# Beginning of a two-layer encoder trunk on one Trainium2 core: x in eight pieces, the first two weight units in halves and computed together, the third unit's split weights in other buffers

## The chip, the cores and the metric

The kernel runs on one core of a Trainium2 chip. The metric is device time in microseconds for one launch. In this document PE is TensorE, ACT is ScalarE, DVE is VectorE, POOL is GpSimd and SP is SyncE, which issues most of the DMAs.

## The reference

Input x is 512 tokens by 1024 features, float32. There are two layers and a final RMSNorm:

```python
for layer in range(DEPTH):
    h = rms_norm(x, norm_mix[layer])
    if layer % 2 == 0:      # one projection, then a gated linear-attention head group and a
        x = x + mixer_gla_sb(h, ab_w_in[i], ab_w_gate2[i], ab_b_gate[i], ab_gla_norm[i], ab_w_out[i])
    else:                   # stick-breaking group; or windowed attention with sinks and a bias
        x = x + mixer_swa(h, c_w_qkv[i], c_sinks[i], c_w_out[i], rel_bias)
    h = rms_norm(x, norm_ffn[layer])
    x = x + conv_ffn(h, ffn_w_up[layer], ffn_conv_w[layer], ffn_conv_b[layer], ffn_w_down[layer])
return rms_norm(x, norm_final)

def rms_norm(x, g):
    return x * lax.rsqrt(jnp.mean(x * x, axis=-1, keepdims=True) + EPS) * g
```

This case touches only the start of layer 0: `rms_norm` and the first of the 25 weight units of `h @ ab_w_in[0]`, namely the first 128 columns each of the stick-breaking q and k (`("qb", 0)`, `("kb", 0)`) and a quarter of its v (`("vb", 0)`).

## The kernel before, in words

**Layout.** x is held transposed, as `x[128, 8, 512]`: eight chunks of 128 features, each with 512 tokens in a row. Weights come in units of 128x1024 float32 (512 KB). A q or k unit is "stationary": eight 128x128 blocks, one per chunk of x. A v unit is "moving": two chunks of weight rows with 512 columns each.

**Three products for one.** Every product is computed as three float32r matmuls. A tensor t is split into `hi` (an ACT copy to float32r) and `lo` (DVE: t minus hi), and hi*hi + hi*lo + lo*hi is accumulated in PSUM; the function is `three`, lines 1160 to 1162. A unit makes 24 matmuls of 512 columns. A weight unit u is loaded by SP into `w_raw[u % 4]`, split by ACT into `w_hi[u % 2]` and by DVE into `w_lo[u % 2]`. Because there are two split buffers, ACT waits for `unit_done` to reach u - 1 before it writes unit u (`hi`, line 599 to 601); DVE's part is `lo` (line 840).

**The norm.** The projection works on x times gain, without 1/rms: ACT writes `h_hi` (line 632), DVE `h_lo` (line 855). Meanwhile the row sums of squares are built: ACT squares the eight chunks (`sq`, line 651), DVE adds each into `ssq` (`add_sq`, line 850), PE sums `ssq` over the partitions (`ssq_mm`, line 1206), and DVE, POOL and PE turn that into `rinv` (lines 873, 588, 877, 1213), by which results are scaled as they leave PSUM.

**Order.** `mix0_order` makes one list of steps, `SEQ0`, and PE, ACT and DVE each walk it and do their part of each step. A step `("unit", u, (a, b))` is eighths a to b of a unit. Behind the last eighth of unit u, `with_splits` puts a step `("split", u)`, at which ACT and DVE split unit u + 2. Before the change the list begins: q's chunks 0 to 3, k's chunks 0 to 3, squares of chunks 0 to 3, q's chunks 4 to 7 and split 0, squares of 4 to 7, k's chunks 4 to 7 and split 1, the whole unit vb 0 and split 2, then `ssq`. The two first units (q, k) are split ahead of the list by two loops over the chunks, on ACT (lines 624 to 632) and on DVE (lines 883 to 886).

**Loads.** At the start SP issues weight unit 0, x chunks 0 and 1, weight unit 1, x chunks 6 and 7, weight units 2 and 3; ACT issues all small parameters (`par`, 202 KB) and then x chunks 2 and 3, and 4 and 5. A row of the table of DMAs below is one of these. PE runs 14 matmuls on a constant (line 1278) while it waits. A queue works through its own DMAs in order; both queues share the 16 DMA engines. Unit 4 and later wait for `w_lo_ready`.

Of the kernel before, what the change touches and what calls it, by code (L numbers as in the profile page):

```python
# [27 lines left out]
F32 = mybir.dt.float32  # L28
# [3 lines left out]
ALU = mybir.AluOpType  # L32
# [3 lines left out]
T = 512  # L36
# [82 lines left out]
def mix0_order():  # L119
# [3 lines left out]
    def ev(name, i=0):  # L123
        return [(name, i, None)]
# [10 lines left out]
    q, k = unit("qb"), unit("kb")  # L135
    seq = q[:4] + k[:4] + ev("sq", 0) + q[4:] + ev("sq", 1) + k[4:]
    seq += unit("vb", 0) + ev("ssq") + cut("vb", 1, 6, "rinv")
# [95 lines left out]
def trunk(nc, xT, w_mix0, w_mix1, w_up, w_down, small, wg2, bias, out):  # L233
    ctx = ExitStack()
    with ctx:
# [3 lines left out]
        def sem(name):  # L239
            return ctx.enter_context(nc.semaphore(name))  # L240
# [24 lines left out]
        def s0(name, shape, dt=F32):  # L265
            return sb(name, shape, dt, m0)
# [20 lines left out]
        sbH = s0("sbH", [P, ZN], F32R)  # L287
        sbL = s0("sbL", [P, ZN], F32R)
        gE = s0("gE", [P, TT * GH * GK])
        gL = s0("gL", [P, TT * GH * GK])  # L290
# [57 lines left out]
        unit_done = sem("unit_done")  # L348
        x_loaded = [sem(f"x_loaded{i}") for i in range(4)]
        par_loaded = sem("par_loaded")  # L350
# [134 lines left out]

        def x_pair(i):
            return xT[:, 2 * i * T:(2 * i + 2) * T].rearrange("p (c t) -> p c t", t=T)

# [18 lines left out]
        def _(sp):  # L507
# [7 lines left out]

            for u in range(RAW):
                sp.dma_start(w_raw[u][:, :], w_mix0[u]).then_inc(w_loaded[u], 16)
                if u < 2:
                    i = 3 * u
                    sp.dma_start(x[:, 2 * i:2 * i + 2, :], x_pair(i)).then_inc(x_loaded[i], 16)  # L520
            sp.dma_start(wg2_sb[:, :], wg2).then_inc(wg2_loaded, 16)
# [72 lines left out]
        def _(act):  # L594
# [23 lines left out]

            act.dma_start(par[:, :], small).then_inc(par_loaded, 16)
            for i in (1, 2):  # L620
                act.dma_start(x[:, 2 * i:2 * i + 2, :], x_pair(i)).then_inc(x_loaded[i], 16)


            for c in range(KC):
                if c % 4 == 0:
                    act.wait_ge(w_loaded[c // 4], 16)
                    s.activation(w_hi[c // 4][:, :], w_raw[c // 4][:, :], ACT.Copy).then_inc(w_hi_ready, 1)
                if c == 0:
                    act.wait_ge(par_loaded, 16)
                if c % 2 == 0:  # L630
                    act.wait_ge(x_loaded[c // 2], 16)
                s.activation(h_hi[:, c, :], x[:, c, :], ACT.Copy, scale=gain_at(0, c)).then_inc(hi_ready, 1)


# [6 lines left out]
            for name, i, span in SEQ0:  # L641
                if name == "unit" and span[1] == 8:
                    n, part = MIX0[i]
                    if n in B_PARTS and part == B_PARTS[n] - 1:
                        act.wait_ge(unit_done, i + 1)
                        b_evac({"vb": vb, "va": va, "kg": kg}[n], B_COLS[n], b_tile, a_before(MIX0, i))
                elif name == "split":
                    hi_static(i + SPL)
# [59 lines left out]
            def ffn(layer, norm, u_up, u_dn, r0, next_cols, last):  # L708


                act.wait_ge(warmed, layer)
                s.activation(gelu_warm[:, :], par[:, 0:1], ACT.Gelu_apprx_tanh).then_inc(warmed, 1)

# [120 lines left out]
        def _(dve):  # L834
# [46 lines left out]

            v.memset(ssq[:, :], 0.0).then_inc(ssq_added, 1)
            for c in range(KC):
                if c % 4 == 0:
                    lo_static(c // 4)
                h_lo_part(0, c)
            dve.wait_ge(consts, N_CONSTS)
            v.tensor_copy(ident_bf[:, :], ident[:, :]).then_inc(consts_dve, 1)
# [17 lines left out]
            for name, i, span in SEQ0:  # L906
                if name == "unit" and span[1] == 8:
                    if i >= 2 and MIX0[i][0] not in B_PARTS:
                        a_evac0(i)
                elif name == "split":  # L910
                    lo_static(i + SPL)
# [243 lines left out]
        def _(pe):  # L1155
# [11 lines left out]

            def a_unit(u, r, bank, h_blocks=None, span=(0, KC)):

                if span[0] == 0:  # L1170
                    pe.wait_ge(w_lo_ready, u + 1)
                for c in range(*span):
                    if h_blocks is not None:
                        pe.wait_ge(lo_ready, h_blocks + c + 1)
                    ins = three(ps[:, bank, :], w_blocks(r, c), (h_hi[:, c, :], h_lo[:, c, :]),
                                c == 0, c == KC - 1)
                if span[1] == KC:
                    ins.then_inc(unit_done, 1)

            def b_unit(u, part, parts, tile, n_cols, span=(0, 8), a_taken_by=None):  # L1180
# [5 lines left out]
                for step in range(span[0] * steps // 8, span[1] * steps // 8):  # L1186

                    half, rest = divmod(step, steps // 2)
                    k, tt = rest // 2, 3 - 2 * half - rest % 2
                    c = part * blocks + k  # L1190
                    if a_taken_by is not None and c == 0 and tt == 1:
                        pe.wait_ge(a_taken, a_taken_by)
                    tok = slice(tt * P, (tt + 1) * P)

                    ins = three(tile(tt, n_cols), (h_hi[:, c, tok], h_lo[:, c, tok]), w_blocks(u % RAW, k, n_cols),
                                c == 0 and (tile is b_tile or tt % 2 == 1), c == KC - 1, tile is v_tile)
# [84 lines left out]
            for at, (name, i, span) in enumerate(SEQ0):  # L1281
                if name == "unit":
# [10 lines left out]
                    else:  # L1293
                        if a >= 4 and span[0] == 0:
                            pe.wait_ge(a_taken, a - 1)
                        if b_done and span[0] == 0:
                            after_group = MIX0[i - 1][0] in B_PARTS
                            pe.wait_ge(b_taken, b_done - TT + 1 if after_group else b_done)
                        a_unit(i, i, a_bank0(a), 0 if i < 2 else None, span)
                elif name == "ssq":  # L1300
# [266 lines left out]
```

## Time and profile before

| | us |
|---|---|
| median of 3 runs | 1163.75 (1162.48 to 1165.25) |
| the profiled execution, its own time | 1162.42 |
| its span in the trace | 1160.7 |
| PE busy in the span | 1127.6 (97%) |
| DVE busy, ACT busy | 653.8 (56%), 492.8 (42%) |

The span leaves out 1.7 us around it. Busy time of PE includes the overlap of pipelined matmuls (a 512-column matmul is shown as 0.39 us long, and the next one starts 0.23 us later), so starts, not durations, tell the pace.

### The profile page before, as it was taken

The page shows a single profiled execution, that of the slowest core. Times are in us where ns is not written, and L with a number is a line of the kernel's source. Part 1 is how long each engine was busy: PE and PEld are TensorE (multiplying, and loading weights), DVE is VectorE, ACT ScalarE, POOL GpSimd, SP SyncE. Part 2 cuts the span into 40 slices and gives each one's busy share as a digit, 9 for nine tenths or more (in the row PEclk, how much of TensorE's full clock was granted, in tenths as well). Part 3 has the DMA queues.
Part 4 walks back from the last instruction along what each step waited for, and adds up shares of the span by engine and source line. Part 5 has one row for each costly group of instructions (what it writes and reads, how often), then busy time and mean ns, then how long its engine had stood idle before and what let it go on. Part 6 is the DMA issues. An engine that isn't in the chain of part 4 may idle for free.

```text
span 1160.7 us, 15078 instructions
## 1 busy us (share of the span) xinstructions
PE 1127.6 (97%) x5402; PEld 918.6 (79%) x5402; DVE 653.8 (56%) x837; ACT 492.8 (42%) x714; POOL 8.6 (1%) x25
## 2 busy tenths in 40 slices
PE   8999999999999999999999999899999999999995
PEld 7776777778888888888888777688888888888884
DVE  6324343565777777774333565655777777763333
ACT  5547354843434434443332365634443443432220
POOL 1000000000000000000000000000000000000000
PEclk9999899999999999999999999999999999999997
DMA  5211111122232232223333222132222223233331
GB/s 225 73 55 55 55 55 55 55 91 91 91 107 92 90 106 93 90 77 94 94 99 120 98 73 89 38 104 89 98 90 103 95 90 106 77 85 93 97 86 72
DMA packets 31751, 102.92 MB, mean 89 GB/s; under 512 B 3537, under 2 KB 3682, under 8 KB 31714
## 3 DMA queue, kind: packets, MB, share of 16 engines
q1 hardware_dynamic: 30978, 100.17, 26.2%
q10 hardware_dynamic: 736, 2.24, 0.6%
q8 instruction: 25, 0.41, 0.1%
q14 instruction: 12, 0.10, 0.0%
HBM read 99.84 MB, written 2.10 MB: 88 GB/s over the span
## 4 chain that ended last, share of the span: by engine, by line
PE 59%; issue 32%; ACT 5%; DVE 4%; DMA 1%; POOLq 0%; POOL 0%; ACTq 0%; DVEq 0%; SPq 0%
PE ps L1160 17%; PE ps L1162 17%; PE ps L1161 17%; PE ps L1324 2%; PE ps L1311 2%; ACT pr L817 1%; ACT w_hi L601 1%; PE ps L1333 1%; DVE w_lo L840 1%; DMA x<-xT 1%; PE ps L1456 1%; DVE sc L1111 1%; ACT sbE L663 0%; DVE mx L1121 0%; DVE x L1148 0%
## 5 line engine op out<-in xcount | busy, mean ns | idle before, releaser
L601 ACT ACTIVATE w_hi<-w_raw 128x1024 fp32r<-128x1024 f32 (+1 forms) x203 | 198.1, 976 | 512.9 <-PE ps L1162 512.9
L840 DVE TENSOR_TENSOR w_lo<-w_raw,w_hi 128x1024 fp32r<-128x1024 f32 (+1 forms) x205 | 229.8, 1121 | 243.7 <-ACT w_hi L601 237.8
L1160 PE MATMUL ps<-h_hi,w_hi 128*128 128x512 f32 x896 | 355.6, 397 | 8.2 <-DVE h_lo L855 3.1
L1162 PE MATMUL ps<-h_hi,w_lo 128*128 128x512 f32 x896 | 349.6, 390 | 0.0
L1161 PE MATMUL ps<-h_lo,w_hi 128*128 128x512 f32 x896 | 349.6, 390 | 0.0
L1160 PEld LDWEIGHTS ps<-h_hi,w_hi 128*128 128x128 f32 x896 | 168.6, 188 | 48.1 <-issue 11.6
L1162 PEld LDWEIGHTS ps<-h_hi,w_lo 128*128 128x128 f32 x896 | 168.6, 188 | 35.4
L1161 PEld LDWEIGHTS ps<-h_lo,w_hi 128*128 128x128 f32 x896 | 168.7, 188 | 35.0 <-issue 1.2
L1160 PE MATMUL ps<-y_hi,w_hi 128*128 128x512 f32 x352 | 136.9, 389 | 0.0
L1161 PE MATMUL ps<-y_lo,w_hi 128*128 128x512 f32 x352 | 136.9, 389 | 0.0
L1162 PE MATMUL ps<-y_hi,w_lo 128*128 128x512 f32 x352 | 136.9, 389 | 0.0
L988 DVE TENSOR_TENSOR us<-ps,rinv 128x512 f32<-128x512 f32 x88 | 60.7, 692 | 84.7 <-PE ps L1162 84.7
L1160 PEld LDWEIGHTS ps<-y_hi,w_hi 128*128 128x128 f32 x352 | 66.1, 188 | 13.8
L1162 PEld LDWEIGHTS ps<-y_hi,w_lo 128*128 128x128 f32 x352 | 66.1, 188 | 13.8
L1161 PEld LDWEIGHTS ps<-y_lo,w_hi 128*128 128x128 f32 x352 | 66.1, 188 | 13.5
L998 DVE SCALAR_TENSOR_TENSOR cv<-us,par,cv 128x512 f32<-128x512 f32 x88 | 66.2, 752 | 11.0 <-DVE cv L995 0.6
L725 ACT ACTIVATE cv<-us,par 128x512 f32<-128x512 f32 x88 | 70.6, 804 | 2.9 <-DVE us L988 2.9
L995 DVE SCALAR_TENSOR_TENSOR cv<-us,par,cv 128x512 f32<-128x512 f32 x88 | 65.6, 746 | 0.6 <-ACT cv L725 0.6
L861 DVE TENSOR_TENSOR x<-ps,x 128x512 f32<-128x512 f32 (+1 forms) x32 | 22.1, 691 | 56.2 <-PE ps L1162 56.2
L1160 PE MATMUL ps<-w_hi,h_hi 128*128 128x512 f32 (+2 forms) x128 | 45.3, 354 | 2.7 <-DVE kbT L900 2.6
L1162 PE MATMUL ps<-w_hi,h_lo 128*128 128x512 f32 (+2 forms) x128 | 43.8, 342 | 0.0
L1161 PE MATMUL ps<-w_lo,h_hi 128*128 128x512 f32 (+2 forms) x128 | 43.8, 342 | 0.0
(181 smaller groups left out, 1050.6 us busy)
## 6 DMA issues: line engine op xcount, KB each, us to landing
w_raw<-w_up SPq DMA_DIRECT2D x88, 512.0 KB, 3.2
w_raw<-w_mix SPq DMA_DIRECT2D x53, 512.0 KB, 3.3
w_raw<-w_down SPq DMA_DIRECT2D x32, 384.0 KB, 3.1
w_raw<-w_down SPq DMA_DIRECT2D x32, 320.0 KB, 2.9
out<-x SPq DMA_DIRECT2D x8, 256.0 KB, 2.2
x<-xT SPq DMA_DIRECT2D x2, 512.0 KB, 8.0
x<-xT ACTq DMA_DIRECT2D x2, 512.0 KB, 8.7
bias_sb<-bias ACTq DMA_DIRECT2D x1, 512.0 KB, 3.9
```

The costliest lines, as they stand in the source:

```text
L601: s.activation(w_hi[r % SPL][:, 0:cols], w_raw[r][:, 0:cols], ACT.Copy).then_inc(w_hi_ready, 1)
L725: s.activation(cv[k % 4][:, :], us[k % 2][:, 2:2 + T], ACT.Identity, bias=par[:, bass.ds(taps + 3, 1)], scale=par[:, bass.ds(taps + 2, 1)] ...
L840: v.tensor_tensor(w_lo[r % SPL][:, 0:cols], w_raw[r][:, 0:cols], w_hi[r % SPL][:, 0:cols].bitcast(F32), ALU.subtract).then_inc(w_lo_ready, 1)
L861: v.tensor_tensor(blk(x, c), ps[:, bank, :], blk(x, c), ALU.add).then_inc(x_updated, 1)
L988: v.tensor_tensor(us[k % 2][:, 2:2 + T], ps[:, k, :], rinv[:, :], ALU.mult).then_inc(u_scaled, 1)
L995: v.scalar_tensor_tensor(cv[k % 4][:, :], us[k % 2][:, 1:1 + T], par[:, bass.ds(taps + 1, 1)], cv[k % 4][:, :], ALU.mult, ALU.add).then_in ...
L998: v.scalar_tensor_tensor(cv[k % 4][:, :], us[k % 2][:, 0:T], par[:, bass.ds(taps, 1)], cv[k % 4][:, :], ALU.mult, ALU.add).then_inc(conv2, 1)
L1160: mm(dst, w[0], m[0], start=first, stop=False, skip_group_check=shared)
L1161: mm(dst, w[0], m[1], start=False, stop=False, skip_group_check=shared)
L1162: return mm(dst, w[1], m[0], start=False, stop=last, skip_group_check=shared)
L1311: mm(zs[:, ZOFF[b]:ZOFF[b] + ZW[b]], kbT[rows, j, b * P:(b + 1) * P], qbT[rows, j, b * P:T], start=b != 3, stop=False, skip_group_check=True)
L1324: ins = mm(dst, lhs[:, :], part[:, ZOFF[c]:ZOFF[c] + ZW[c]], start=False, stop=c == TT - 1 and part is sbL, skip_group_check=True)
```

## The change

The eight chunks of x get a DMA and a semaphore each. The first two weight units are loaded, split on ACT and DVE, and waited for by PE in two halves of 128x512 (four blocks each). The order of issue on SP becomes: first halves of units 0 and 1, x chunks 2 and 3, second half of unit 0, chunk 4, second half of unit 1, chunks 5, 6, 7, units 2 and 3. ACT issues chunk 0, the gains (44 of the 404 columns of `par`), chunk 1, and the other 360 columns of `par` behind the split of unit 2. PE works q and k chunk by chunk. Unit 2 is split into the first 1024 columns of `sbH` and `sbL`, which the attention uses only later, so that its split waits for no matmul and stands ahead of the list; split 0 drops out of it. Both `sq` steps now stand behind the last chunk of both units.

```diff
-    seq = q[:4] + k[:4] + ev("sq", 0) + q[4:] + ev("sq", 1) + k[4:]
+    seq = sum((q[c:c + 1] + k[c:c + 1] for c in range(KC)), []) + ev("sq", 0) + ev("sq", 1)
...
+        third_hi, third_lo = sbH[:, 0:UC], sbL[:, 0:UC]
...
+        def load_x(engine, c):
+            engine.dma_start(x[:, c, :], xT[:, c * T:(c + 1) * T]).then_inc(x_loaded[c], 16)
+        def load_half(engine, u, half):
+            engine.dma_start(w_raw[u][:, W_HALVES[half]], w_mix0[u][:, W_HALVES[half]]).then_inc(
+                w_loaded[u] if half else half_loaded[u], 16)
...
-            for u in range(RAW):
+            load_half(sp, 0, 0)
+            load_half(sp, 1, 0)
+            for c in (2, 3):
+                load_x(sp, c)
+            load_half(sp, 0, 1)
+            load_x(sp, 4)
+            load_half(sp, 1, 1)
+            for c in (5, 6, 7):
+                load_x(sp, c)
+            for u in (2, 3):
                 sp.dma_start(w_raw[u][:, :], w_mix0[u]).then_inc(w_loaded[u], 16)
-                if u < 2:
-                    i = 3 * u
-                    sp.dma_start(x[:, 2 * i:2 * i + 2, :], x_pair(i)).then_inc(x_loaded[i], 16)
...
-            act.dma_start(par[:, :], small).then_inc(par_loaded, 16)
-            for i in (1, 2):
-                act.dma_start(x[:, 2 * i:2 * i + 2, :], x_pair(i)).then_inc(x_loaded[i], 16)
+            load_x(act, 0)
+            act.dma_start(par[:, 0:S_CONV], small[:, 0:S_CONV]).then_inc(gains_loaded, 16)
+            load_x(act, 1)
+            def half_hi(u, half):
+                act.wait_ge(w_loaded[u] if half else half_loaded[u], 16)
+                s.activation(w_hi[u][:, W_HALVES[half]], w_raw[u][:, W_HALVES[half]],
+                             ACT.Copy).then_inc(w_hi_ready if half else half_hi_ready, 1)
             for c in range(KC):
-                if c % 4 == 0:
-                    act.wait_ge(w_loaded[c // 4], 16)
-                    s.activation(w_hi[c // 4][:, :], w_raw[c // 4][:, :], ACT.Copy).then_inc(w_hi_ready, 1)
+                if c % 4 < 2:
+                    half_hi(c % 4, c // 4)
                 if c == 0:
-                    act.wait_ge(par_loaded, 16)
-                if c % 2 == 0:
-                    act.wait_ge(x_loaded[c // 2], 16)
+                    act.wait_ge(gains_loaded, 16)
+                act.wait_ge(x_loaded[c], 16)
                 s.activation(h_hi[:, c, :], x[:, c, :], ACT.Copy, scale=gain_at(0, c)).then_inc(hi_ready, 1)
+            act.wait_ge(w_loaded[SPL], 16)
+            s.activation(third_hi, w_raw[SPL][:, :], ACT.Copy).then_inc(w_hi_ready, 1)
+            act.dma_start(par[:, S_CONV:S_END], small[:, S_CONV:S_END]).then_inc(par_loaded, 16)
...
-                elif name == "split":
+                elif name == "split" and i > 0:
                     hi_static(i + SPL)
```

DVE gets the same pattern (half splits in the loop over chunks, then `third_lo`, and `split` only for i > 0). On PE, `a_unit` waits for `half_lo_ready` ahead of chunk 0 and for `w_lo_ready` ahead of chunk 4 of the first two units, and `b_unit` reads unit 2 from the third pair of buffers.

The places that matter, engine by engine. On ACT, from the last `h_hi` to the copy of `rinv`, before:

```order
L632 ACTIVATE h_hi<-x,par 128x512
L651 ACTIVATE va<-x 128x512 x4
L601 ACTIVATE w_hi<-w_raw 128x1024 [waits unit_done,w_loaded2]
L651 ACTIVATE raT<-x 128x512 x4
L601 ACTIVATE w_hi<-w_raw 128x1024 [waits unit_done,w_loaded3]
L601 ACTIVATE w_hi<-w_raw 128x1024 [waits unit_done,w_loaded0]
L617 ACTIVATE rinv<-ps 128x512 [waits rbc_done]
```

and now:

```order
L654 ACTIVATE h_hi<-x,par 128x512 [waits x_loaded7]
L656 ACTIVATE sbH<-w_raw 128x1024 [waits w_loaded2]
L657 DMA par<-small 128x360
L620 ACTIVATE w_hi<-w_raw 128x1024 [waits unit_done,w_loaded3]
L676 ACTIVATE va<-x 128x512 x4
L676 ACTIVATE raT<-x 128x512 x4
L620 ACTIVATE w_hi<-w_raw 128x1024 [waits unit_done,w_loaded0]
L636 ACTIVATE rinv<-ps 128x512 [waits rbc_done]
```

`va` and `raT` are where the squares are kept. Four squares stood ahead of the first split that waits for PE, and all eight stand behind one now; that split is unit 3's, which waits for `unit_done` to be 2, the end of both first units.

On DVE, the same stretch, before:

```order
L850 TENSOR_TENSOR ssq<-ssq,va 128x512 [waits ssq_added,sq_ready] x4
L840 TENSOR_TENSOR w_lo<-w_raw,w_hi 128x1024 [waits w_hi_ready]
L850 TENSOR_TENSOR ssq<-ssq,raT 128x512 [waits ssq_added,sq_ready] x4
L840 TENSOR_TENSOR w_lo<-w_raw,w_hi 128x1024 [waits w_hi_ready] x2
L873 TENSOR_SCALAR var_col<-ps 128x4 [waits ssq_col]
```

and now:

```order
L921 TENSOR_TENSOR sbL<-w_raw,sbH 128x1024 [waits w_hi_ready]
L866 TENSOR_TENSOR w_lo<-w_raw,w_hi 128x1024 [waits w_hi_ready]
L876 TENSOR_TENSOR ssq<-ssq,va 128x512 [waits ssq_added,sq_ready] x4
L876 TENSOR_TENSOR ssq<-ssq,raT 128x512 [waits ssq_added,sq_ready] x4
L866 TENSOR_TENSOR w_lo<-w_raw,w_hi 128x1024 [waits w_hi_ready]
L899 TENSOR_SCALAR var_col<-ps 128x4 [waits ssq_col]
```

The `w_lo` of unit 3 stands ahead of all eight additions; that of unit 4 stays between them and `var_col`.

On PE the sum over `ssq` has kept its place, behind the 24 matmuls of unit 2. The first matmuls now:

```order
L1195 MATMUL ps<-h_hi,w_hi0 128x512 [waits lo_ready,half_lo_ready]
L1196 MATMUL ps<-h_lo,w_hi0 128x512
L1197 MATMUL ps<-h_hi,w_lo0 128x512
L1195 MATMUL ps<-h_hi,w_hi1 128x512 [waits lo_ready,half_lo_ready]
L1196 MATMUL ps<-h_lo,w_hi1 128x512
L1197 MATMUL ps<-h_hi,w_lo1 128x512
L1195 MATMUL ps<-h_hi,w_hi0 128x512 [waits lo_ready]
```

Before, twelve matmuls with `w_hi0` came first and then twelve with `w_hi1`; now the two units take turns after every three.

## Rows read from the trace of the kernel before

**Rows 1.** The page, part 1 (busy us, share, instructions).
```profile
PE 1127.6 (97%) x5402; PEld 918.6 (79%) x5402; DVE 653.8 (56%) x837; ACT 492.8 (42%) x714; POOL 8.6 (1%) x25
```

**Rows 2.** PE's waits, whole span (us in total, times, longest us).
```profile
PE ps L1160 <- DVE h_lo L855: 3.1, 1, 3.1
PE ps L1160 <- DVE kbT L900: 2.6, 1, 2.6
...
PE ps L1360 <- ACT gE L680: 1.8, 1, 1.8
```

**Rows 3.** Timeline of PE (start us, us, instruction), from the first units to the norm.
```profile
1.38 4.88 PE L1278 MATMUL ps<-ones 128*128 128x128 f32 x28 [1.38 <-POOL ones L564]
9.37 0.47 PE L1160 MATMUL ps<-h_hi,w_hi 128*128 128x512 f32 x1 [3.11 <-DVE h_lo L855]
12.56 0.50 PE L1160 MATMUL ps<-h_hi,w_hi 128*128 128x512 f32 x1 [0.21 <-DVE w_lo L840]
17.91 0.39 PE L1162 MATMUL ps<-h_hi,w_lo 128*128 128x512 f32 x1
20.63 0.39 PE L1162 MATMUL ps<-h_hi,w_lo 128*128 128x512 f32 x1
26.35 0.94 PE L1206 MATMUL ps<-ones,ssq 128*128 128x1 f32 x8
31.38 1.02 PE L1213 MATMUL ps<-sq,ones 128*128 128x512 f32 x2
```

**Rows 4.** Timeline of ACT, the same stretch.
```profile
5.35 1.06 ACT L627 ACTIVATE w_hi<-w_raw 128x1024 fp32r<-128x1024 f32 x1 [1.83 <-DMA w_raw<-w_mix]
7.71 2.56 ACT L632 ACTIVATE h_hi<-x,par 128x512 fp32r<-128x512 f32 x4 [1.31 <-DMA x<-xT]
18.39 1.06 ACT L601 ACTIVATE w_hi<-w_raw 128x1024 fp32r<-128x1024 f32 x1 [2.25 <-PE ps L1162]
19.36 2.19 ACT L651 ACTIVATE raT<-x 128x512 f32<-128x512 f32 x4
```

**Rows 5.** Timeline of DVE, the same stretch.
```profile
8.47 2.74 DVE L855 SCALAR_TENSOR_TENSOR h_lo<-x,par,h_hi 128x512 fp32r<-128x512 f32 x4 [0.81 <-ACT h_hi L632]
...
19.48 1.23 DVE L840 TENSOR_TENSOR w_lo<-w_raw,w_hi 128x1024 fp32r<-128x1024 f32 x1 [0.93 <-ACT w_hi L601]
20.63 3.08 DVE L850 TENSOR_TENSOR ssq<-ssq,raT 128x512 f32<-128x512 f32 x4
23.62 1.22 DVE L840 TENSOR_TENSOR w_lo<-w_raw,w_hi 128x1024 fp32r<-128x1024 f32 x1
```

**Rows 6.** DMA packets from 0 to 3.0, 3.6, 4.5, 4.8, 8 and 12 us.
```profile
DMA packets 49, 0.16 MB, mean 55 GB/s; under 512 B 0, under 2 KB 15, under 8 KB 49
DMA packets 96, 0.31 MB, mean 86 GB/s; under 512 B 0, under 2 KB 34, under 8 KB 96
DMA packets 239, 0.68 MB, mean 152 GB/s; under 512 B 9, under 2 KB 113, under 8 KB 239
DMA packets 291, 0.80 MB, mean 166 GB/s; under 512 B 23, under 2 KB 145, under 8 KB 291
DMA packets 651, 2.09 MB, mean 261 GB/s; under 512 B 63, under 2 KB 191, under 8 KB 651
DMA packets 1104, 3.75 MB, mean 312 GB/s; under 512 B 112, under 2 KB 240, under 8 KB 1104
```

**Rows 7.** The page, part 6: DMA issues (count, KB each, median us to landing).
```profile
w_raw<-w_mix SPq DMA_DIRECT2D x53, 512.0 KB, 3.3
```

**Rows 8.** Timeline of SP's queue, its first DMA.
```profile
0.81 0.39 SPq L517 DMA_DIRECT2D w_raw<-w_mix  x1
```

**Rows 9.** Windows: busy us (count) of PE, PEld, DVE, ACT, POOL; granted clock; DMA.
```profile
10.00:15.00 5.00, 4.79 (x22) 3.65 (x21) 4.93 (x7) 4.76 (x8) 0.00 (x0) 1.00 1.02 413
70.00:72.00 2.00, 2.00 (x9) 2.00 (x10) 0.95 (x1) 0.00 (x0) 0.00 (x0) 0.50 0.00 0
120.00:123.00 3.00, 3.00 (x9) 2.42 (x10) 0.42 (x1) 0.18 (x1) 0.00 (x0) 0.50 0.53 175
```

More of the change, by code:

```diff
@@ L348, in trunk @@
         unit_done = sem("unit_done")
-        x_loaded = [sem(f"x_loaded{i}") for i in range(4)]
+        x_loaded = [sem(f"x_loaded{c}") for c in range(KC)]
+        gains_loaded = sem("gains_loaded")
+        half_loaded = [sem(f"half_loaded{u}") for u in range(2)]
+        half_hi_ready = sem("half_hi_ready")
+        half_lo_ready = sem("half_lo_ready")
         par_loaded = sem("par_loaded")
@@ L484, in trunk @@
         NADD = KC + 1
-        def x_pair(i):
-            return xT[:, 2 * i * T:(2 * i + 2) * T].rearrange("p (c t) -> p c t", t=T)
+        W_HALVES = (slice(0, UC // 2), slice(UC // 2, UC))
+        def load_x(engine, c):
[3 more added lines that the diff above has]
+                w_loaded[u] if half else half_loaded[u], 16)
         def o1_psum(b):
@@ L711, in ffn @@
                 act.wait_ge(warmed, layer)
+                act.wait_ge(par_loaded, 16)
                 s.activation(gelu_warm[:, :], par[:, 0:1], ACT.Gelu_apprx_tanh).then_inc(warmed, 1)
@@ L882, in _, with half_lo @@
             v.memset(ssq[:, :], 0.0).then_inc(ssq_added, 1)
+            def half_lo(u, half):
+                dve.wait_ge(w_hi_ready if half else half_hi_ready, u + 1)
+                cols = W_HALVES[half]
+                v.tensor_tensor(w_lo[u][:, cols], w_raw[u][:, cols], w_hi[u][:, cols].bitcast(F32),
+                                ALU.subtract).then_inc(w_lo_ready if half else half_lo_ready, 1)
             for c in range(KC):
-                if c % 4 == 0:
-                    lo_static(c // 4)
+                if c % 4 < 2:
+                    half_lo(c % 4, c // 4)
                 h_lo_part(0, c)
+            dve.wait_ge(w_hi_ready, SPL + 1)
+            v.tensor_tensor(third_lo, w_raw[SPL][:, :], third_hi.bitcast(F32), ALU.subtract).then_inc(w_lo_ready, 1)
             dve.wait_ge(consts, N_CONSTS)
@@ L909, in _ @@
                         a_evac0(i)
-                elif name == "split":
+                elif name == "split" and i > 0:
                     lo_static(i + SPL)
@@ L1166, in w_blocks, with third_blocks, a_unit @@
                 return tuple(t[r % SPL][:, c * n:(c + 1) * n] for t in (w_hi, w_lo))
-            def a_unit(u, r, bank, h_blocks=None, span=(0, KC)):
-                if span[0] == 0:
+            def third_blocks(c, n):
+                return tuple(t[:, c * n:(c + 1) * n] for t in (third_hi, third_lo))
+            def a_unit(u, r, bank, h_blocks=None, span=(0, KC), in_halves=False):
+                if in_halves and span[0] == 0:
+                    pe.wait_ge(half_lo_ready, u + 1)
+                if span[0] == (KC // 2 if in_halves else 0):
                     pe.wait_ge(w_lo_ready, u + 1)
@@ L1193, in b_unit @@
                     tok = slice(tt * P, (tt + 1) * P)
-                    ins = three(tile(tt, n_cols), (h_hi[:, c, tok], h_lo[:, c, tok]), w_blocks(u % RAW, k, n_cols),
+                    ins = three(tile(tt, n_cols), (h_hi[:, c, tok], h_lo[:, c, tok]),
+                                third_blocks(k, n_cols) if u == SPL else w_blocks(u % RAW, k, n_cols),
                                 c == 0 and (tile is b_tile or tt % 2 == 1), c == KC - 1, tile is v_tile)
@@ L1298, in _ @@
                             pe.wait_ge(b_taken, b_done - TT + 1 if after_group else b_done)
-                        a_unit(i, i, a_bank0(a), 0 if i < 2 else None, span)
+                        a_unit(i, i, a_bank0(a), 0 if i < 2 else None, span, i < 2)
                 elif name == "ssq":
```

## The prediction

> **What bounds the kernel now.** I read the page first: PE is busy 97% of the span [rows 1], so a beginning that starts PE sooner shortens the kernel one for one, unless PE waits again soon after. Then PE's own waits: they are few, and the longest, 3.1 us, is at the very start, for the first `h_lo` [rows 2]. Then the timelines of PE, ACT and DVE in the first 32 us [rows 3 to 5]. PE's 14 warming matmuls end at 6.26 us, the first real one starts at 9.37, the last one of the first two units at 20.63, the sum over `ssq` at 26.35 and the matmul for `rinv` at 31.38; past 9.37 there is one gap of 0.21 us. What ends the wait at 9.37 is x: ACT waits for it until 7.71, and PE follows 1.66 us later (`h_hi`, `h_lo`, handing over) [rows 3, 4].
>
> The change acts on two things: when PE starts, and what the norm's sum waits for.
>
> **Part 1: the first matmul.** It needs the first half of unit 0, chunk 0 and the gains, then a half split, `h_hi` and `h_lo`. The trace shows no such small DMAs. What it shows is that a 128-row DMA leaves 144 packets, and that 291 packets had gone by 4.8 us, those of unit 0 and `par` [rows 6]; ACT used unit 0 at 5.35 [rows 4], some 0.5 us behind. The first half and chunk 0 are again 288 packets with fewer bytes (0.52 MB against 0.73), so they land between 4.6 (by bytes: 0.52 MB had gone a little after 4.0) and 5.3. The gains come second on ACT's queue and share the engines with the first half of unit 1. By bytes they need 0.8 MB, which had gone at 4.8, so they land at 5.3. By packets they are 288 more behind the first 288, at 173 per us (239 to 291 in 0.3 us) 1.7 us, so 7.0. I take the middle, 6.15: the gains' packets are tiny, and nothing shows what one costs. First matmul: 6.15 + 1.66 = 7.8 us. The ends: 6.0 us, if the half unit lands in the 3.0 us or so that whole units take later (3.3 in the median, [rows 7]), from issue at 0.81 [rows 8], with half a copy (0.55) and the 1.66 behind it; and 7.0 + 1.66 = 8.6.
>
> **Part 2: q and k together.** The matmuls are the same 48. 36 of them took 20.63 - 12.56 = 8.07 us from first to last start, 0.231 us each [rows 3]; 47 steps are 10.85 us. ACT's and DVE's work for one chunk (`h_hi` 0.64 us, `h_lo` 0.69 us, a quarter of the four-packs of [rows 4, 5], and four half splits in all) stays under PE's six matmuls, 1.38 us, so PE is not held by them once it runs. The last matmul of the second unit starts at 7.8 + 10.85 = 18.65, against 20.63: 2.0 us sooner. Chunk 7 must land by 18.65 - 5 x 0.231 - 1.66 = 15.8. It is the 13th DMA, 1872 packets. From 49 packets at 3.0 us that asks for 1823 in 12.3 us (0.5 for landing), or 148 per us. Rows of 4 KB went at 113 per us (651 to 1104 in 4 us), which is 415 GB/s, while the mixture of 4 KB and 1.6 KB rows went at 159 per us (96 to 239 in 0.9 us), at the same bytes per us [rows 6]. So bytes are the limit down to that size, and 2 KB rows should do 180 to 200 per us: chunk 7 lands near 13.5, unit 2 near 15. I take nothing for it; the other end is rival 2.
>
> The Trainium skill (DMA: Bandwidth & Descriptors, section Bandwidth) speaks against such pieces: it wants DMAs of 1 MiB or more for three quarters of the peak. Its fit of a fixed 2.0 us plus bytes over 436 GB/s (same page, Anatomy of one DMA) gives 2.6 us for a 256 KB piece; as an estimate, ten of them one after another on SP's queue would end at 27 us and starve PE. The trace disagrees for pieces of 512 KB: queued behind one another they moved 413 GB/s [rows 9]. No row shows 256 KB ones.
>
> **Part 3: the third unit's buffers.** The 0.2 us that PE had between its second and third unit goes. Unit 2 is split by 15 + 1.1 + 1.3 = 17.4, over a microsecond before PE wants it at 18.9. Worth 0 to 0.2 us, but it is taken up by the next part.
>
> **Part 4: the squares.** This decides. ACT walks its list in order, and its split of unit 3 waits for the end of both units. Before, four squares stood ahead of the first split, that waited for unit 0 only; the last of the other four additions was over at 23.7, and PE asked for it at 26.35, 2.6 us later. Now all eight stand behind that wait. From the last matmul of unit 1 (call its start L) the chain is worked out from the same steps around unit 0:
> - ACT's split starts 18.39 - 17.91 = 0.48 behind the start of the unit's last matmul [rows 3, 4];
> - DVE's part starts 19.48 - 18.39 = 1.09 later, and the first addition 20.63 - 19.48 = 1.15 after that [rows 4, 5];
> - eight additions: 4 take 23.62 - 20.63 = 2.99 [rows 5], 8 take 5.98, and 0.16 for the end of the last and handing over. The squares keep ahead of them: they start 0.97 behind the split and come every 0.52 us, an addition every 0.75.
>
> Sum: L + 0.48 + 1.09 + 1.15 + 5.98 + 0.16 = L + 8.86. PE has unit 2's 24 matmuls to do in between and would ask at L + 5.72 (26.35 - 20.63) [rows 3]. So it waits 3.1 us, with nothing else in its queue that could go ahead, since PE takes its instructions in order. That gives back 3.1 us where 2.0 were won. The sum over `ssq` starts at 7.8 + 10.85 + 8.86 = 27.5 against 26.35: 1.16 us later than before. Everything behind hangs on it with the old distances: the `w_lo` of unit 4 that stood ahead of `var_col` is now out of the way sooner, but `rinv`'s matmul at 31.38 stands behind 18 matmuls of unit 3 anyway and did not wait. The ends of the first matmul make this -0.6 to +2.0.
>
> **Part 5: PE's clock.** A new idle stretch of 3.0 us stands in the middle of full work. After PE's waits of 2.6 and 1.8 us [rows 2] it ran slower: in the windows behind them the granted clock is 0.50, 1.2 GHz [rows 9]. There a 512-column matmul came every 0.43 us and not every 0.23 (nine in three microseconds against 22 in five), and some eight came so, 1.6 us lost. I take that; the ends are 0 and, as the stretch might last twice as long, 3. After the 3.1 us at the start the clock was 1.00 in this execution [rows 9]; the change shortens that stretch to 1.5 us, which gains only in executions where it fell there. The Trainium skill (TensorE: Matmul & The Clock Gate, Part 1) says that the number of slow matmuls differs from run to run of one kernel. By it the fall is a matter of chance in each execution, and the median may hold one at the start.
>
> **Sum**, against the profiled execution's own 1162.42 us: -1.98 (front) + 3.14 (the wait for the squares) + 1.6 (clock) = +2.76, or 1165.2. The median of the runs shown is 1.3 above that execution; I add none of this, as a clock fall at the start, which would explain it, is what the change takes away. Against the median it is +1.4 us, or 0.12%.
>
> **Rivals.**
> 1. The clock does not fall in the new stretch: 1162.4 + 1.2 = 1163.6, to 1164.9 from the median. For it: the 3.1 us stretch at the start left the clock alone. Against: it came behind two others, and shorter ones.
> 2. Slower: small rows starve the front. If a 2 KB packet takes as long as a 4 KB one (113 per us), chunk 7 lands at 3.0 + 1823/113 + 0.5 = 19.6, the last matmul of unit 1 starts at 19.6 + 1.66 + 1.16 = 22.4, 1.8 later than before, and the wait for the squares comes on top: +4.9, or 1167.3 to 1168.7, with PE's gaps in the front. It decides from 148 packets per us downwards. Against: the 159 per us of mixed rows. The skill's rule above would bring it about.
> 3. Faster: the squares don't hold PE, and the front's gain stays. It takes additions over by L + 5.7, which the order on ACT and DVE speaks against; with a first matmul at 6.8 it would be 1163.75 - 3.0 = 1160.8.
>
> **Chances.** Forecast 0.57 (own range 1163.9 to 1166.6), rival 1 0.22, rival 2 0.12, rival 3 0.09. Time 1165.2, range 1162.7 to 1167.2: below lies rival 3, above most of rival 2. Within 0.2% of 1163.75, about what a measurement can tell, is 1161.4 to 1166.1. Faster: rival 3 and a tail, 0.09. Slower: rival 2 and a sixth of the forecast, 0.22. Same: 0.69.
>
> **What would show it.** In the changed kernel's trace: the first real matmul at 6.8 to 8.6 us, with the gains' DMA as what ACT waited for last; no wait of PE over 0.3 us up to the end of unit 1; all eight additions behind the `w_lo` of unit 3; a PE wait of about 3 us for `ssq` at the sum; granted clock 0.50 in the 3 us behind it. I am wrong if that wait is under 1.5 us, if PE stands still for x within the first units, or if something past 32 us moves by itself.

## The result, and the profile after

| | before | after |
|---|---|---|
| median of 20 runs each | 1163.71 us (1162.28 to 1165.25) | 1166.17 us (1164.95 to 1167.33) |
| profiled execution, its own time | 1162.42 | 1166.02 |
| its span | 1160.7 | 1164.3 |

The ratio is 1.0025, with a 95% interval of 1.0019 to 1.0031: the change made the kernel slower by 2.5 us. Between the two profiled executions it is 3.6 us, and the difference of these two numbers is one of the things to explain.

PE's longest waits in the kernel after, to be held against [rows 2] (us in total, times, longest us):

```profile
PE ps L1248 <- DVE ssq L876: 5.3, 2, 3.1
...
PE ps L1195 <- DVE kbT L935: 2.6, 1, 2.6
...
PE ps L1195 <- DVE h_lo L881: 1.2, 1, 1.2
```

The wait for `h_lo` at the start has shrunk from 3.1 to 1.2 us. A new one of 3.1 us stands at the sum over `ssq` (the other 2.2 of that row is the last norm's, as before). The timeline of PE shows where (start us, us, instruction), beside [rows 3]:

```profile
1.38 5.54 PE L1320 MATMUL ps<-ones 128*128 128x128 f32 x28 [1.38 <-POOL ones L583]
8.08 0.47 PE L1195 MATMUL ps<-h_hi,w_hi 128*128 128x512 f32 x1 [1.17 <-DVE h_lo L881]
...
18.86 0.39 PE L1197 MATMUL ps<-h_hi,w_lo 128*128 128x512 f32 x1
...
27.98 1.02 PE L1248 MATMUL ps<-ones,ssq 128*128 128x1 f32 x8 [3.14 <-DVE ssq L876]
...
34.68 1.02 PE L1255 MATMUL ps<-sq,ones 128*128 128x512 f32 x2
```

The last matmul of the first two units starts at 18.86, 1.8 us sooner than the 20.63 of before, with no gap in between. The sum starts at 27.98, 1.6 later than before, and `rinv`'s matmul at 34.68, 3.3 later. What ACT does in that time, by its timeline (beside [rows 4, 5]):

```profile
6.42 0.72 ACT L654 ACTIVATE h_hi<-x,par 128x512 fp32r<-128x512 f32 x1 [1.30 <-DMA par<-small]
...
19.34 1.06 ACT L620 ACTIVATE w_hi<-w_raw 128x1024 fp32r<-128x1024 f32 x1 [4.67 <-PE ps L1197]
20.31 2.18 ACT L676 ACTIVATE va<-x 128x512 f32<-128x512 f32 x4
```

And the timeline of DVE behind it:

```profile
20.43 1.23 DVE L866 TENSOR_TENSOR w_lo<-w_raw,w_hi 128x1024 fp32r<-128x1024 f32 x1 [4.10 <-ACT w_hi L620]
21.58 3.08 DVE L876 TENSOR_TENSOR ssq<-ssq,va 128x512 f32<-128x512 f32 x4
24.76 3.08 DVE L876 TENSOR_TENSOR ssq<-ssq,raT 128x512 f32<-128x512 f32 x4
```

ACT stands idle for 4.67 us, and DVE for 4.10, with all eight chunks of x long in use (the last `h_hi` ends at 13.25), until PE is through the second unit; only then come the squares. The window behind the sum (busy us and count of PE, PEld, DVE, ACT, POOL; granted clock; DMA):

```profile
30.00:33.00 3.00, 3.00 (x9) 2.32 (x8) 0.69 (x1) 0.00 (x0) 0.38 (x1) 0.50 0.47 175
```

Nine matmuls touch these three microseconds, at a granted clock of 0.50, as in [rows 9]; their starts are 0.43 us apart (30.36, 30.79, 31.21) where they were 0.23 apart ahead of the wait. In the windows beside it, 27 to 30 and 33 to 36, the clock is 0.97 and 0.96. So it was low from 29.8 to 33.2, and the fall began 1.8 us after PE had gone back to work.

### The profile page after: what moved, and what is told of

It reads as the page before. It is cut to its first block, busy times and chain, and to the rows that moved or that the text cites. A ratio compares the mean times of both kernels' runs of the same rounds, so it can differ in the third digit from the quotient of the medians.

```text
span 1164.3 us, 15092 instructions
## 1 busy us (share of the span) xinstructions
PE 1130.0 (97%) x5402; PEld 920.4 (79%) x5402; DVE 654.0 (56%) x839; ACT 493.0 (42%) x716; POOL 8.6 (1%) x25
## 4 chain that ended last, share of the span: by engine, by line
PE 59%; issue 32%; ACT 4%; DVE 4%; DMA 1%; ACTq 0%; POOLq 0%; POOL 0%; DVEq 0%
PE ps L1195 17%; PE ps L1197 17%; PE ps L1196 17%; PE ps L1366 2%; PE ps L1353 2%; ACT pr L843 1%; ACT w_hi L620 1%; PE ps L1375 1%; DVE w_lo L866 1%; PE ps L1498 1%; DVE sc L1146 1%; DVE ssq L876 0%; ACT sbE L688 0%; DMA par<-small 0%; DVE mx L1156 0%
## 5 line engine op out<-in xcount | busy, mean ns | idle before, releaser
L866 DVE TENSOR_TENSOR w_lo<-w_raw,w_hi 128x1024 fp32r<-128x1024 f32 (+1 forms) x202 | 226.1, 1119 | 239.2 <-ACT w_hi L620 238.3
L1195 PE MATMUL ps<-w_hi,h_hi 128*128 128x512 f32 (+2 forms) x120 | 42.2, 352 | 2.7 <-DVE kbT L935 2.6
L1196 PE MATMUL ps<-w_lo,h_hi 128*128 128x512 f32 (+2 forms) x120 | 41.1, 342 | 0.0
L1197 PE MATMUL ps<-w_hi,h_lo 128*128 128x512 f32 (+2 forms) x120 | 41.0, 342 | 0.0
```

The lines of the kernel that those rows point to most:

```text
L866: v.tensor_tensor(w_lo[r % SPL][:, 0:cols], w_raw[r][:, 0:cols], w_hi[r % SPL][:, 0:cols].bitcast(F32), ALU.subtract).then_inc(w_lo_ready, 1)
L1195: mm(dst, w[0], m[0], start=first, stop=False, skip_group_check=shared)
L1196: mm(dst, w[0], m[1], start=False, stop=False, skip_group_check=shared)
L1197: return mm(dst, w[1], m[0], start=False, stop=last, skip_group_check=shared)
```

## The experiments

Every experiment was timed against the kernel before on its own chip; that kernel's median was 1163.76 us in experiments 1 to 4, 1163.59 in 5 to 8 and 1163.61 in 9 to 12. They are numbered in the order in which they were made and told by subject, so 12 stands beside 6, and 11 beside 10. The kernel after was not timed beside them, so comparisons with it go by traces first. The theory: the squares stand behind a split that waits for PE, and the wait which this gives PE also costs clock. The rivals: the new front itself costs something, or the clock falls by chance.

**1. Squares ahead of the wait** (in the changed kernel).

```diff
-    seq = sum((q[c:c + 1] + k[c:c + 1] for c in range(KC)), []) + ev("sq", 0) + ev("sq", 1)
+    seq = (sum((q[c:c + 1] + k[c:c + 1] for c in range(KC - 1)), []) + ev("sq", 0) + ev("sq", 1)
+           + q[KC - 1:] + k[KC - 1:])
```

> The changed kernel with both steps of squares moved ahead of the last eighth of the second unit, so that on ACT and DVE all eight squares and additions stand ahead of unit 3's split and wait for no matmul. Theory (the squares stand behind a wait for PE): the first matmul stays at 8.1 us, the sum over ssq is asked for and done at 24.7 instead of 27.98, no wait there, granted clock 1.00 behind it, rinv's matmul at 29.7 instead of 34.68. Time 1161.6 to 1162.3, that is about 1.6 to 2 us under the kernel before. Rival (the third unit's extra split or the small pieces cost something later): the wait goes but the time stays above 1163. Rival (the chain after the sum takes its place): rinv's matmul waits for DVE, at 30 or later.

Measured: 1160.55 us, ratio 0.9974 (0.9964 to 0.9983). Timeline of its PE:

```profile
8.06 0.47 PE L1196 MATMUL ps<-h_hi,w_hi 128*128 128x512 f32 x1 [1.31 <-DVE h_lo L882]
24.64 0.95 PE L1249 MATMUL ps<-ones,ssq 128*128 128x1 f32 x8
29.68 1.02 PE L1256 MATMUL ps<-sq,ones 128*128 128x512 f32 x2
```

And of its DVE, the two groups of additions:

```profile
16.27 3.08 DVE L877 TENSOR_TENSOR ssq<-ssq,va 128x512 f32<-128x512 f32 x4
19.44 3.08 DVE L877 TENSOR_TENSOR ssq<-ssq,raT 128x512 f32<-128x512 f32 x4
```

The wait is gone, the additions are over 2 us before PE asks, and nothing took its place: `rinv`'s matmul is 5.0 us sooner than in the changed kernel and 1.7 sooner than before. All places are where the theory put them, and both rivals fall. The time fell further than expected: 3.2 us under the kernel before, where 1.6 to 2 were expected.

Part of the excess stands in this trace, behind the norm. The profiled execution took 1159.34, 3.1 us less than that of the kernel before, though `rinv`'s matmul was only 1.7 sooner. 1.3 of the rest come at PE's wait for `kbT`, which ends at 68.21 here. It is 2.62 us long as before, but this time the granted clock stayed at 1.00 behind it. Experiment 11 is the same kernel; there the same wait of 2.62 us ends at 68.30, and the clock fell. The window from 69 to 72 us, here and there:

```profile
69.00:72.00 3.00, 3.00 (x23) 2.91 (x23) 0.29 (x1) 0.00 (x0) 0.00 (x0) 1.00 0.46 162
69.00:72.00 3.00, 3.00 (x13) 2.81 (x13) 0.38 (x1) 0.00 (x0) 0.00 (x0) 0.51 0.45 152
```

So one and the same wait costs clock in one execution and none in another. The ten executions of this kernel fall into two groups of five, 1159.34 to 1160.14 and 1160.95 to 1161.66, and its median lies between them. Experiments 6, 9 and 12 bear on another part, some 1.0 us.

**2. The kernel before with the squares behind.**

```diff
-    seq = q[:4] + k[:4] + ev("sq", 0) + q[4:] + ev("sq", 1) + k[4:]
+    seq = q[:4] + k[:4] + q[4:] + k[4:] + ev("sq", 0) + ev("sq", 1)
```

> The kernel before with only the two steps of squares moved behind the second unit; loads, halves and buffers as before. Theory: first matmul at 9.37 and last of unit 1 at 20.63 as before; ACT's split of unit 3 at 21.1, additions from 23.35 to 29.4, sum over ssq at 29.5 instead of 26.35 (+3.15), then a fall of the clock (+1.6): about 1168.2. Rival (the wait comes from the new front, not from the squares): no change from 1163.7.

Measured: 1168.76 us, ratio 1.0048 (1.0034 to 1.0061). PE's timeline:

```profile
29.75 1.84 PE L1206 MATMUL ps<-ones,ssq 128*128 128x1 f32 x8 [3.26 <-DVE ssq L850]
37.61 1.02 PE L1213 MATMUL ps<-sq,ones 128*128 128x512 f32 x2
```

And three windows there (columns as above):

```profile
27.00:30.00 3.00, 0.25 (x2) 0.28 (x2) 2.69 (x5) 0.64 (x1) 0.00 (x0) 0.80 0.00 0
30.00:33.00 3.00, 3.00 (x12) 2.71 (x13) 1.39 (x4) 0.00 (x0) 1.02 (x1) 0.50 0.38 93
33.00:36.00 3.00, 3.00 (x10) 2.34 (x8) 0.69 (x1) 0.00 (x0) 0.00 (x0) 0.56 0.22 87
```

One moved pair of steps makes the same wait in a kernel with the old front: 3.3 us, and the sum 3.4 later. The slow stretch was twice as long here. By the shares of these windows the clock was low from 28.8 to 35.6 us, 6.8 in all, where it was 29.8 to 33.2, 3.4 in all, after the change. From the sum to `rinv`'s matmul it is 7.86 us, against 5.03 before and 6.70 after the change, so the clock cost 2.8 us here and 1.7 there, about half of the slow time in which PE had work. Why one stretch was twice the other stays open. The rival (no change) fell.

**3. Work for PE in the wait** (in the changed kernel).

```diff
+        FILL = 10
...
                 elif name == "ssq":
+                    for _ in range(FILL):
+                        mm(ps[:, B_RINV, 0:P], ones[:, :], ones[:, :], start=True, stop=True)
                     ssq_mm(0)
```

> The changed kernel with ten more matmuls on the constant (128x128, float32, into a PSUM bank that is free then) just ahead of the sum over ssq, so that PE works through most of its wait of 3.1 us. Theory (an idle stretch costs clock): the sum stays at 28.0, granted clock 1.00 from 28 to 34, rinv's matmul at about 33.1 instead of 34.68, time 1164.2 to 1164.7, 1.6 under the changed kernel. Rival (the clock falls for another reason, or by chance whatever PE does): slow matmuls behind 28 us as before, 1166.2.

Measured: 1163.26 us, its profiled execution 1164.42. PE's timeline:

```profile
28.15 1.02 PE L1249 MATMUL ps<-ones,ssq 128*128 128x1 f32 x8 [0.90 <-DVE ssq L877]
33.24 1.02 PE L1256 MATMUL ps<-sq,ones 128*128 128x512 f32 x2
```

And the window behind the wait:

```profile
31.00:34.00 3.00, 3.00 (x14) 2.22 (x12) 0.27 (x1) 0.00 (x0) 0.00 (x0) 1.00 0.30 122
```

The sum comes as late as before behind the first units (28.15 - 19.02 = 9.13 us after their last matmul's start, against 9.12), but of the wait only 0.90 us is idle. The clock stays at 1.00, and from the sum to `rinv`'s matmul it is 5.09 us again. The profiled executions differ by 1.60 (1166.02 - 1164.42), just the size expected; the medians, not taken side by side, by 2.9, more than expected. All eleven executions (1162.52 to 1164.75) lie under the fastest of the changed kernel's twenty (1164.95), so it is not one lucky profile.

**4. The gains first on ACT's queue** (in the changed kernel).

```diff
-            load_x(act, 0)
             act.dma_start(par[:, 0:S_CONV], small[:, 0:S_CONV]).then_inc(gains_loaded, 16)
+            load_x(act, 0)
```

> The changed kernel with the DMA of the gains issued ahead of chunk 0 on ACT's queue. Theory (ACT waits for the gains last, since they come second on their queue): first h_hi at 5.5 to 5.9 instead of 6.42, first matmul at 7.2 to 7.6 instead of 8.08, and everything behind earlier by the same, 0.5 to 0.9 us, the wait for the squares unchanged at 3.1: 1165.3 to 1165.7. Rival (packets in all decide, not their order): no change.

Measured: 1167.43 us (1166.02 to 1171.09), no gain. ACT's first `h_hi`:

```profile
6.67 0.72 ACT L654 ACTIVATE h_hi<-x,par 128x512 fp32r<-128x512 f32 x1 [1.57 <-DMA x<-xT]
```

It waits for chunk 0 now, and until 6.67, not 6.42: the rival (no change) was right. The gains themselves did land sooner when first, 3.8 us after their issue at 0.82 and not 5.1 after 1.28, that is at 4.6 and not 6.4; but `h_hi` needs both, and whichever of the two stands second on the queue comes at about 6.4 to 6.7. This fits a count of packets in all, though no run varies that count alone. In the changed kernel 406 packets had gone at 4.8 us and 719 at 6.0, about as many as five DMAs have (144 each); before, it was 291 at 4.8. DMA packets from 0 to 4.8, 6, 8 and 10 us of the changed kernel:

```profile
DMA packets 406, 0.71 MB, mean 147 GB/s; under 512 B 64, under 2 KB 64, under 8 KB 406
DMA packets 719, 1.09 MB, mean 182 GB/s; under 512 B 197, under 2 KB 197, under 8 KB 719
DMA packets 1106, 1.79 MB, mean 224 GB/s; under 512 B 242, under 2 KB 242, under 8 KB 1106
DMA packets 1554, 2.61 MB, mean 261 GB/s; under 512 B 292, under 2 KB 292, under 8 KB 1554
```

From 4.8 to 6.0 us, with the gains' 176-byte rows among them, 261 packets went per microsecond; from 8 to 10 us it was 224 per us, 199 of them 2 KB rows, or 410 GB/s, the rate of 4 KB rows (415) [rows 6]. Why the median lies 1.3 above the changed kernel's, which was not timed beside it, stays open; two of its seven executions, 1169.19 and 1171.09, lie far above the others, and its profile (1166.36) is not one of them.

**5. The old list in the changed kernel.** Its `seq` line is that of the kernel before, the line that experiment 2 takes out.

> The changed kernel with the list of steps of the kernel before (four chunks of one unit, then four of the other, the squares between): pieces, halves and the third unit's buffers stay. Theory (only the place of the squares was wrong, and the chunk order is worth what chunk 3 comes later than chunk 0): squares ahead of the wait, no wait for the sum. PE needs chunks 1 to 3 after 0.69 us each and h_lo comes every 0.7 with one half split of 0.69 among them, so up to 0.7 us of gaps in the first units; otherwise as with the squares ahead: 1160.5 to 1161.4. Rival (turn by turn of the two units is what won the front): first units end at 19.8 or later, 1161.8 or more.

Measured: 1161.66 us, ratio 0.9983 (0.9974 to 0.9992). No wait for the sum, which starts at 25.72; PE waits 0.82 us for the second chunk's `h_lo` at 9.76. So the old order of steps in the new front beats both kernels, and taking the units by turns is worth 1.1 us more: 25.72 - 24.64 in the traces, 1161.66 - 1160.55 in the medians (of two chips). Both expectations held in part. The last matmul of the first two units starts at 19.89, where the rival had put it (19.8 or later); the time lies between the theory's 1161.4 and the rival's 1161.8. Of the 1.8 us that the front wins, the turns are 1.0 (19.89 - 18.86).

**6 and 12. More warming matmuls in the kernel before.**

```diff
-        WARM = 14
+        WARM = 23
```

> The kernel before with 23 warming matmuls in place of 14, so that PE works until about 9 us and the stretch of 3.1 us is filled. Theory (the median of the kernel before holds a clock fall behind that stretch in many executions, which its profiled one had not): median 1162.2 to 1163.0, 0.8 to 1.6 under the kernel before. Rival (no fall there; the spread of the kernel before comes from later waits): 1163.5 to 1163.9, unchanged.

Measured: 1162.56 us, ratio 0.9995 (0.9986 to 1.0004). Once more, since that interval holds 1:

> The sixth experiment once more (the kernel before with 23 warming matmuls), whose interval of 0.9986 to 1.0004 did not part the two theories. Theory (clock falls at the start are in the median of the kernel before): 1162.5, about 1.1 under it. Rival (chance): 1163.6.

Measured: 1162.57 us, ratio 0.9991 (0.9982 to 1.0000). Two medians 1.03 and 1.04 us under the kernel before. Each interval by itself still holds 1; together the executions are clearer. Of the 59 of the kernel before on these two chips, 41 took more than 1163.2 us; of the 22 with the stretch filled, one did. Filling the first stretch is worth about 1 us of the median. That a fall of the clock is what it saves fits, but no trace of the kernel before holds such a fall.

**7. More warming with the squares ahead** (`WARM = 18`).

> The changed kernel with the squares moved ahead (as in the first experiment) and 18 warming matmuls in place of 14, so that the 1.3 us ahead of the first matmul are filled. Theory (an idle stretch of 1.3 us does not touch the clock): as the first experiment, 1160.4 to 1160.8. Rival (its better and worse executions, 1159.4 and 1161.0, differ by a fall there): median 1159.5.

Measured: 1160.89 us, and its executions fall into two groups as in experiment 1 (four from 1159.58 to 1159.78, seven from 1160.85 to 1161.32). PE has no wait left ahead of the first matmul, so the groups don't come from the first stretch. What does fit is the wait for `kbT` at 68 us: the profiled executions of the slower groups (1160.85 here, 1161.02 in experiment 11) have the fall behind it, and that of the faster group (1159.34 in experiment 1) has not. Three profiles make this likely; they don't show it.

**8. The gains by POOL, squares ahead.**

```diff
             load_x(act, 0)
-            act.dma_start(par[:, 0:S_CONV], small[:, 0:S_CONV]).then_inc(gains_loaded, 16)
...
             step(g.memset(ones[:, :], 1.0))
+            pool.dma_start(par[:, 0:S_CONV], small[:, 0:S_CONV]).then_inc(gains_loaded, 16)
```

> The squares moved ahead, and the gains' DMA issued by POOL behind its memset of the constant instead of second by ACT: a third queue. Theory (the gains wait for their turn behind chunk 0 on ACT's queue): gains land by 5.6, first h_hi follows chunk 0 at 5.5 to 5.8 instead of 6.41, first matmul at 7.3, 1159.8. Rival (three queues share the engines, and what is ahead of the gains in all of them counts): h_hi at 6.2 to 6.6, 1160.5, or later, since POOL issues more slowly.

Measured: 1164.01 us (1162.17 to 1165.48). The gains come later, not sooner: POOL issues them at 1.62, `h_hi` waits for them until 7.70, and the first matmul starts at 9.36 behind an idle stretch of 2.98 us. The later start explains 1.3 us of the 3.5 over the first experiment (3.1 over the seventh, on the same chip). The profiled execution, 1162.17, is the fastest of the eleven, and its clock stayed at 1.00 behind that stretch.

**9. The same with that stretch filled** (`WARM = 23`).

> The eighth experiment (squares ahead, gains issued by POOL, first matmul at 9.4 us behind an idle stretch of 3.0 us, median 1164.0) with 23 warming matmuls in place of 14, so that this stretch is filled. Theory (a stretch of 3 us at the start costs a clock fall in most executions, though none in the profiled ones): median 1161.9 to 1162.4, that is the first experiment's 1160.6 plus the 1.3 us by which the first matmul is later, and none above 1163.5. Rival (POOL's DMA itself costs the rest): 1164.0 as before.

Measured: 1161.85 us, ratio 0.9989 (0.9980 to 0.9998), one of eleven executions above 1163.5 (1164.63). First matmul at 9.52, the sum at 26.11 against 25.94. Nine additional matmuls on a constant took 2.2 us off the median, though they made every place in the first 31 us 0.16 later. The theory was "none above 1163.5"; six of eleven were above it in the eighth experiment. So the stretch of 3 us costs time in many executions, and that of the profile was not one of them. That this time is clock is inferred; the slow start shown next is the one trace that holds such a fall.

**11 and 10. The first experiment again, and with work in the last two waits.**

```diff
+            for _ in range(6):
+                mm(ps[:, 0, 0:P], ones[:, :], ones[:, :], start=True, stop=True)
             ssq_mm(2 * LAYERS)
+            for _ in range(6):
+                mm(ps[:, 0, 0:P], ones[:, :], ones[:, :], start=True, stop=True)
             rinv_mm(2 * LAYERS)
```

> The first experiment once more, on this chip, for comparison with the two ahead of it: 1160.5, between 1159.3 and 1161.7.

> The first experiment (squares ahead) with six more matmuls on the constant ahead of each of the last two matmul groups of the kernel (the last sum over ssq and the last rinv), where PE stands idle for 2.2 and 2.1 us. Theory (the clock falls behind these stretches too): granted clock 1.00 to the end, the rinv matmul 1.02 us long instead of 2.08 and the sum 0.95 instead of 1.21, 1159.3 to 1159.6 (1.0 to 1.3 under the first experiment). Rival (the additional matmuls come too late or the fall is already there): 1160.5 or more.

Measured: 1160.26 us, ratio 0.9974 (0.9964 to 0.9983), without the additional work; 1160.01, ratio 0.9968 (0.9956 to 0.9981), with it. The last matmul group in the timeline of PE, without the additional work:

```profile
1149.13 2.07 PE L1256 MATMUL ps<-sq,ones 128*128 128x512 f32 x2 [2.07 <-DVE sq L904]
```

And with it:

```profile
1150.81 1.12 PE L1256 MATMUL ps<-sq,ones 128*128 128x512 f32 x2 [0.62 <-DVE sq L904]
```

It is 0.95 us shorter, about as expected (1.06), while the sum ahead of it stayed at 1.05 us. The median moved by 0.25 only, with intervals that overlap; the expected 1159.3 to 1159.6 was missed, and whether the whole is worth more than nothing is not shown. The profiled execution with the additional work, 1161.76, was the slowest of its six (the others 1158.81 to 1160.14) and shows by luck what the profile of the kernel before did not. The edit at the end does not touch the start. PE's timeline there:

```profile
8.36 0.64 PE L1196 MATMUL ps<-h_hi,w_hi 128*128 128x512 f32 x1 [1.85 <-DVE h_lo L882]
8.81 0.63 PE L1197 MATMUL ps<-h_lo,w_hi 128*128 128x512 f32 x1
9.23 0.63 PE L1198 MATMUL ps<-h_hi,w_lo 128*128 128x512 f32 x1
```

And the window:

```profile
8.00:11.00 3.00, 2.64 (x7) 2.09 (x8) 2.89 (x6) 2.83 (x5) 0.00 (x0) 0.58 1.05 406
```

Here the clock did fall behind the first idle stretch, of 1.85 us. The sum came at 26.54 instead of 24.64: 0.3 us of this is the later first matmul (8.36 against 8.06), 1.6 is clock.

## Why the prediction was right, step by step

The measured 1166.17 lies within the stated range, 1.0 above the forecast of 1165.2, and the mechanism is the forecast one: part 4's wait for the squares, with part 5's clock behind it, eats more than the front wins. The likeliest answer, no change within 0.2%, was missed by a little: the interval of 1.0019 to 1.0031 is mostly above that line.

- **First matmul** (part 1): forecast 7.8, measured 8.08. ACT did wait for the gains last, until 6.42. From there it took the forecast 1.66. The middle between the count by bytes and the count by packets was 0.27 too early. The step's reason, that they come second on their queue, was half the truth: with the gains first, chunk 0 came last at 6.67 (experiment 4), and from POOL's queue the gains came at 7.70 (experiment 8).
- **The two units by turns** (part 2): 18.86 - 8.08 = 10.78 us, forecast 10.85. No PE wait for x. 2 KB rows moved at the rate of 4 KB rows, 410 GB/s against 415, so rival 2 fell. The rule on DMAs of 1 MiB or more (the Trainium skill, DMA: Bandwidth & Descriptors, section Bandwidth) does not hold for 256 KB pieces queued one behind another on SP and ACT; 410 GB/s stand against it. The fit that the prediction took from the same page of the Trainium skill (Anatomy of one DMA) is given there for DMAs issued by GpSimd, so the estimate of 27 us applied it to queues that it was not measured on.
- **The third unit's buffers** (part 3): the prediction misread its row. The gap of 0.21 us in [rows 3] stands at 12.56, ahead of the second unit and for its `w_lo`; from the second unit to the third PE had no gap (20.63, 20.85). With the second unit split in halves that gap is gone. The new buffers have another use that the prediction did not name. By turns, unit 0's last matmul starts at 18.18, and a split of unit 2 that waited for it would be done 2.7 us later (0.48 + 1.09 + 1.15, part 4), at 20.9, while PE went on to unit 2 at 19.08. That is an estimate from these rows; no run has the turns without the buffers.
- **The squares** (part 4): forecast 8.86 us behind the last matmul's start, measured 27.98 - 18.86 = 9.12. ACT's start (0.48), DVE's (1.09) and the first addition (1.15) came just as forecast; 0.19 of the 0.26 is the step from the first four additions to the next four (24.76 - 21.58 = 3.18, forecast 2.99), 0.07 the rest. So the sum came 3.40 us later behind the first units than before (9.12 - 5.72), where 3.14 was forecast. That the trace also shows an idle time of 3.14 is a coincidence: it is counted from the modelled end of the last matmul, not from the moment when PE would have started the sum. The first experiment takes it away, the second makes it in the old kernel: this step is shown from both sides. Rival 3 (the squares don't hold PE) fell.
- **The clock** (part 5): forecast 1.6, measured 6.70 - 5.03 = 1.67; the third experiment gives it back and leaves the sum as late as it was. That the size came out so near is partly luck: the second experiment shows 2.8 behind such a wait, near the 3 that the prediction gave as its upper end, and the first shows nothing lost behind a wait of 2.62. The spacing of 0.43 us that the step works with does not follow from the nine in three microseconds that it quotes, which make 0.33, since they include matmuls that only touch the window and small ones; it is in the timeline of the kernel before (starts at 120.83, 121.26 and 121.69).
- **The sum**, profile against profile: forecast +2.76, traces at `rinv`'s matmul +3.30: front -1.77 (forecast -1.98), squares +3.40 (3.14), clock +1.67 (1.6). The remaining 0.3 come between 73 and 94 us, behind the wait for `kbT`: the lag is 3.31 where that wait ends (73.18 against 69.87) and 3.56 at the next wait's end (93.95 against 90.39). The clock falls there in both, for 3.4 us; but before, it fell 0.5 us ahead of the end of the wait (at 69.4), so that part of the slow stretch was idle, and after the change 1.0 us behind it (at 74.2), so that all of it met work. The prediction had set everything past 32 us at nothing.
- **Profile against median**: the prediction added none of the 1.3 us between the profiled execution of before and its median, saying that this may be a clock fall at the start, which the change takes away. That was argued only. The sixth and twelfth experiment (-1.0 each), the ninth against the eighth (-2.2) and the slow start just shown bear it out, though no trace of the kernel before has the fall itself. It also closes the account of the result: +3.6 between profiles, less about 1.0, is +2.6, and the medians say +2.5. The same 1.0 us is part of the 1.2 to 1.6 by which the first experiment beat its expectation; the rest, 0.2 to 0.6, is left open, and the fall at 68 us that comes in some executions only is the likely place.

So the change wins 1.8 us at the front and about 1 us of the median behind the first stretch, and gives back 3.4 us between the last matmul of the two units and the sum (9.12 us now, 26.35 - 20.63 = 5.72 before) and 1.7 us of clock. With two steps of the list moved, the gain stays: 1160.3 to 1160.6 us, 0.26% under the kernel before and 0.5% under the changed one.

## What to carry to other kernels

When an engine walks a list in order, a step that needs nothing must not stand behind one that waits for another engine; a reordered front is worth what the first step with a shared list position lets through, so look up, for every moved step, what now stands ahead of it on each engine. Count an idle stretch of TensorE twice, once as time and once as clock that may be lost behind it (0 to 2.8 us in these traces). And one profile shows one execution: a stretch that left the clock alone there can cost 1 to 2 us in the median.

## What was not expected of the hardware

- A stretch of 3 us with PE idle at the start, behind 14 small matmuls, left the clock at 1.00 in the profiled executions of the kernel before (3.11 us) and of the second (2.89) and eighth experiment (2.98). Filled, it gave 1.0 us of median in the kernel before and 2.2 in the eighth. In one profile a stretch of 1.85 us at the same place halved the clock.
- After the same kind of wait in the same place the clock was low for 3.4 us in one kernel and 6.8 in another, which cost 1.7 and 2.8 us. And one wait of 2.62 us at 68 us had a fall behind it in one execution of a kernel and none in another (experiments 11 and 1), worth 1.5 us between these two traces.
- A DMA of 128 rows of 176 bytes, 22 KB in all, was what ACT waited for last, until 6.4 us, 5.1 us after its issue as second on ACT's queue. First on that queue it took 3.8 us, and issued from POOL 6.1, until 7.7 us.
